# Normalising attention probabilities with a diagonal matmul instead of a transposed inverse, in a two-layer diffusion-transformer trunk

## The reference

```python
def softmax_attend(q, k, v, scale):
    s = jnp.einsum('bqhd,bkhd->bhqk', q, k, preferred_element_type=jnp.float32) * scale
    p = jax.nn.softmax(s, axis=-1).astype(v.dtype)
    return jnp.einsum('bhqk,bkhe->bqhe', p, v)
...
def gqa_sink_attend(q, k, v, sink, scale, mask=None):
    ...
    p = jax.nn.softmax(jnp.concatenate([s, sk], axis=-1), axis=-1)[..., :-1]
    return jnp.einsum('bhgqk,bkhd->bqhgd', p.astype(v.dtype), v)
```

## Time and profile before

| what | value |
|---|---|
| time, median of 3 runs | 4492.41 us (4491.73 to 4493.24) |
| time of the profiled execution | 4492.41 us |
| its span | 4490.5 us |
| instructions | 53404 |
| PE busy | 3760.7 us (84%) |
| DVE busy | 1731.2 us (39%) |
| ACT busy | 1438.4 us (32%) |

### The profile page before, as it was taken

The page is one execution under the profiler, slowest core; times in us unless marked ns, Lnnn a source line. Parts: engine busy times, 40 slices in busy tenths (PEclk is TensorE's granted clock), DMA queues, the critical chain, the costliest instruction groups (busy, mean ns, idle before and its releaser), DMA issues. The chain is left out here.

```text
span 4490.5 us, 53404 instructions
## 1 busy us (share of the span) xinstructions
PE 3760.7 (84%) x19419; PEld 2939.3 (65%) x19419; DVE 1731.2 (39%) x2448; ACT 1438.4 (32%) x2009; POOL 1196.2 (27%) x552
## 2 busy tenths in 40 slices
PE   4969987886869899998999877668867689999897
PEld 0137866776747688887877563346646568888676
DVE  0015211885761322223544404345547513223343
ACT  0035431674540411111322505544434322111222
POOL 0003322423402233332422221121111124444221
PEclk9979988998979999999999989779989899999998
DMA  5761212004423211112544222220010231222345
GB/s 171 268 206 53 69 66 83 24 30 89 101 84 116 81 62 64 61 61 71 199 168 161 70 68 57 71 70 27 27 40 20 84 133 61 79 71 70 128 169 171
DMA packets 330332, 415.65 MB, mean 93 GB/s; under 512 B 68974, under 2 KB 237534, under 8 KB 330046
## 3 DMA queue, kind: packets, MB, share of 16 engines
q1 hardware_dynamic: 300158, 327.40, 23.0%
q10 hardware_dynamic: 30016, 86.16, 5.3%
HBM read 315.95 MB, written 98.04 MB: 92 GB/s over the span
## 5 line engine op out<-in xcount | busy, mean ns | idle before, releaser
L567 PE MATMUL up_acc<-fa_act_h,up_w_hi 128*128 128x512 f32 (+1 forms) x1760 | 651.1, 370 | 27.2 <-DVE fa_act_l L508 27.2
L567 PE MATMUL up_acc<-fa_act_l,up_w_hi 128*128 128x512 f32 (+1 forms) x1760 | 649.5, 369 | 0.0
L567 PE MATMUL up_acc<-fa_act_h,up_w_lo 128*128 128x512 f32 (+1 forms) x1760 | 648.8, 369 | 0.0
L544 POOL TENSOR_TENSOR up_w_hi<-up_w_raw,ONES 128x1024 fp32r<-128x1024 f32 x88 | 210.9, 2396 | 747.0 <-PE up_acc L567 665.2
L962 DVE SCALAR_TENSOR_TENSOR up_conv<-up_acc,PRM,up_conv 128x1023 f32<-128x1023 f32 (+1 forms) x132 | 130.1, 1013 | 692.3 <-ACT up_conv L946 692.3
L567 PEld LDWEIGHTS up_acc<-fa_act_h,up_w_hi 128*128 128x128 f32 x1760 | 333.0, 189 | 87.7 <-issue 19.9
L1054 PE MATMUL dn_acc<-dn_h_hi,dn_w_hi 128*128 128x512 f32 (+1 forms) x880 | 331.6, 377 | 61.1 <-DVE dn_h_lo L1097 59.9
L567 PEld LDWEIGHTS up_acc<-fa_act_h,up_w_lo 128*128 128x128 f32 x1760 | 332.7, 189 | 55.7
L567 PEld LDWEIGHTS up_acc<-fa_act_l,up_w_hi 128*128 128x128 f32 x1760 | 333.1, 189 | 54.9
L946 ACT ACTIVATE up_conv<-up_acc,PRM 128x1280 f32<-128x1280 f32 (+1 forms) x88 | 115.8, 1316 | 767.9 <-PE up_acc L567 767.9
L1054 PE MATMUL dn_acc<-dn_h_lo,dn_w_hi 128*128 128x512 f32 (+1 forms) x880 | 328.8, 374 | 0.0
(11 more groups left out here) (353 smaller groups left out, 7843.7 us busy)
## 6 DMA issues: line engine op xcount, KB each, us to landing
dn_w_raw<-in_ffn_down SPq DMA_DIRECT2D x110, 512.0 KB, 3.3
ada_w<-in_ada_w SPq DMA_DIRECT2D x24, 2048.0 KB, 7.9
up_w_raw<-in_ffn_up SPq DMA_DIRECT2D x88, 512.0 KB, 3.8
dn_h_raw<-H SPq DMA_DIRECT2D x88, 256.0 KB, 3.4
H<-up_conv ACTq DMA_DIRECT2D x22, 640.0 KB, 2.9
H<-up_conv ACTq DMA_DIRECT2D x22, 512.0 KB, 3.5
Y<-qk_ob ACTq DMA_DIRECT2D x17, 640.0 KB, 3.0
na_bias<-RPB SPq DMA_DIRECT2D x80, 128.0 KB, 4.6
```

What stands on the lines that cost most here:

```text
L544: pool.tensor_tensor(W.hi[:, s, :, 0:mw], W.raw[:, s, :, 0:mw], ones[:, 0:mw].unsqueeze(1).broadcast_to([P, W.kt, mw]), ALU.mult)\
L567: t = pe.matmul(acc[0:mw, s, a - t0:b - t0], w[:, s, k, 0:mw], x[:, k, a - a0:b - a0], start=(k == 0 and w is W.hi and x is act_h), stop=( ...
```

## The change

Where `nw` is 2, the tiles `inv` and `inv_t`, the semaphore `spread` and the function `normalize` go. DVE now makes, for each tile and head, a 128x128 matrix `diag` with the reciprocals on its diagonal (identity times the reciprocal, one scalar for each partition). PE's "p" job multiplies each block of `PR` by `diag` in an f32 matmul, where it was a transpose through the identity, so that what comes out is transposed and normalised. It waits for `weighted[e]`, which `diag` raises, where it waited for `exped[e]`. An "o" job is then only the values, and its bank is copied plainly by ACT or DVE according to its parity. In `values` the loop over the two heads is now outside and the loop over the key blocks inside. In da (`nw` is 1) the operations stay as they are.

```diff
--- before.py
+++ after.py
@@ -1157,9 +1157,7 @@
         PR = st.sb("PR", [P, npr, 2, smax])
         PT = st.sb("PT", [P, nw, kmax, 2 * gs * P])
         if nw == 2:
-            NRB = 8
-            inv = st.sb("inv", [P, NRB, P])
-            inv_t = st.sb("inv_t", [P, 2, gs * P])
+            diag = st.sb("diag", [P, 2, 2, P])
         opar = 2
         ob = st.sb("ob", [P, opar, NTL * P])
         stat = st.sb("stat", [P, 2, 8])
@@ -1178,7 +1176,6 @@
         scored, maxed, exped, weighted = st.sems("scored"), st.sems("maxed"), st.sems("exped"), st.sems("weighted")
         t_ready, t_free = st.sems("t_ready", NB), st.sems("t_free", NB)
         chain, sink_exp, inverted = st.sem("chain"), st.sem("sink_exp"), st.sem("inverted")
-        spread = st.sem("spread")
         stored = st.sem("stored")
         block = st.block()
 
@@ -1379,15 +1376,17 @@
                                                 G.IDENT[:, :])
                         last.then_inc(t_ready[bank], 1)
                     else:
-                        if diff:
-                            pe.wait_ge(weighted[e], a + 1)
-                        else:
-                            pe.wait_ge(exped[e], a + 1)
+                        pe.wait_ge(weighted[e], a + 1)
                         t = tiles[a % NTL]
                         for x, k in enumerate(c):
                             col, _, ln = t.kts[k]
-                            last = pe.transpose(tb[0:ln, bank, x * P:(x + 1) * P], PR[:, a % npr, e, col:col + ln],
-                                                G.IDENT[:, :])
+                            w = PR[:, a % npr, e, col:col + ln]
+                            o = tb[0:ln, bank, x * P:(x + 1) * P]
+                            if diff:
+                                last = pe.transpose(o, w, G.IDENT[:, :])
+                            else:
+
+                                last = pe.matmul(o, w, diag[:, a % 2, e, :], start=True, stop=True)
                         last.then_inc(t_ready[bank], 1)
                     job[0] += 1
 
@@ -1406,14 +1405,10 @@
                 c0 = pt_cols(u * NTL + members[0])[0]
                 c1 = c0 + len(members) * P
                 t = tiles[members[0]]
-                if nw == 2:
-                    for y, x in enumerate(range(u * NTL + members[0], m + 1)):
-                        pe.wait_ge(inverted, x + 1)
-                        pe.transpose(tb[:, bank, (gs + y) * P:(gs + y + 1) * P], inv[:, x % NRB, :], G.IDENT[:, :])
-                for k, (_, vt, ln) in enumerate(t.kts):
-                    for e in range(nw):
-                        h = slice(0, P) if diff else slice(e * 64, e * 64 + 64)
-                        vc = slice(u // 2 * 64, u // 2 * 64 + 64) if swa else h
+                for e in range(nw):
+                    h = slice(0, P) if diff else slice(e * 64, e * 64 + 64)
+                    vc = slice(u // 2 * 64, u // 2 * 64 + 64) if swa else h
+                    for k, (_, vt, ln) in enumerate(t.kts):
                         last = pe.matmul(tb[h, bank, 0:c1 - c0], V[0:ln, 0 if swa else u % 2, vt, vc], PT[0:ln, e, k, c0:c1],
                                          start=k == 0, stop=k == len(t.kts) - 1)
                 last.then_inc(t_ready[bank], 1)
@@ -1431,30 +1426,11 @@
                         scores(n, half, jobs[:early(n, half)])
                     turn(jobs[early(n, half):])
 
-        def normalize(eng, copy, gn, bank, use):
-
-            u, g = divmod(gn, len(groups))
-            w = len(groups[g]) * P
-            if copy == "act":
-                eng.wait_ge(t_ready[bank], use + 1)
-                if gn >= 2:
-                    wait_freed(eng, "o", gn - 2)
-                eng.activation(inv_t[:, gn % 2, 0:w], tb[:, bank, gs * P:gs * P + w], ACT.Copy).then_inc(spread, 1)
-                return
-            eng.wait_ge(spread, gn + 1)
-            if u >= opar:
-                eng.wait_ge(stored, 16 * (u - opar + 1))
-            eng.tensor_tensor(ob[:, u % opar, groups[g][0] * P:(groups[g][-1] + 1) * P], tb[:, bank, 0:w],
-                              inv_t[:, gn % 2, 0:w], ALU.mult).then_inc(t_free[bank], 1)
-
         def evacuate(eng, copy, jobs, job):
 
             for what, a, e, c in jobs:
                 bank, use = job[0] % NB, job[0] // NB
                 job[0] += 1
-                if what == "o" and nw == 2:
-                    normalize(eng, copy, a, bank, use)
-                    continue
                 if bank % 2 != (0 if copy == "act" else 1):
                     continue
                 eng.wait_ge(t_ready[bank], use + 1)
@@ -1537,10 +1513,11 @@
                     link(dve.tensor_tensor(s, s, stat[:, p, 6:8], ALU.add))
                 link(dve.reciprocal(s, s))
                 if not diff:
-                    if m >= NRB:
-                        wait_ready(dve, "o", group_no(m - NRB))
-                    dve.tensor_copy(inv[:, m % NRB, :].rearrange("p (e d) -> p e d", e=2),
-                                    s.unsqueeze(2).broadcast_to([P, 2, 64])).then_inc(inverted, 1)
+                    for e in range(2):
+                        if m >= 2:
+                            wait_ready(dve, "p", m - 2, e)
+                        dve.tensor_scalar(diag[:, p, e, :], G.IDENT[:, :], stat[:, p, 2 + e:3 + e], None, ALU.mult)\
+                            .then_inc(weighted[e], 1)
                     return
                 link(dve.tensor_scalar(stat[:, p, 2:3], stat[:, p, 2:3], G.LINV[:, 0:1], None, ALU.mult))
                 dve.tensor_scalar(stat[:, p, 3:4], stat[:, p, 3:4], G.NLAM[:, 0:1], None, ALU.mult).then_inc(inverted, 1)
```

## The result

The changed kernel takes 4644.84 us (median of 4 runs, 4643.67 to 4648.3) against 4492.07 us before (median of 4 runs): a ratio of 1.0342, with a 95% interval of 1.033 to 1.0354. That is 153 us slower where 206 us were forecast, inside the range of 4634 to 4784 us.

The account below looks back on a forecast made before the run. PE was taken to bound the kernel, busy 84% of the span. Its added work, 93.3 us in na, 135.8 in ma and 62.7 in sw, 291.8 together, less 85.5 hidden in idle time, gave 4699 us, range 4634 to 4784.

Parts of the forecast that it names:

- PE bounds the stages: In na, ma and sw PE is busiest, leaving only 114.0 us idle in which extra PE work can hide.
- the second instruction: Probability blocks: each f32 matmul with diag is two PE instructions, 0.110 us more than a transpose, 153.1 us over 1392.
- The exchanged loops: In values, heads outside end the overlap of two heads' matmuls: 48.2 us in na, 68.8 ma, 32.7 sw.
- Rival (a): In values PE overlaps the heads despite the order, or pairs are something else: 4549 us; chance 0.09.
- Three quarters of PE's idle time: In na, ma and sw the added PE work fills 85.5 of 114.0 us idle.
- rival (c): No idle PE time is filled, since waits only move: all 291.8 us added, 4784 us or more; chance 0.05.
- The clock: PE was granted 0.97, 0.95 and 0.93 of full speed in na, ma, sw; at most 36 us to be had.
- (d): PE with fewer gaps keeps full clock and all idle time fills: 4634 us, edge of the main case's 0.82.
- 10.9: PE's 104 transposes of inv in na, ma and sw disappear, giving back 10.9 us.
- DVE and ACT at nothing: Their changed work per tile costs nothing under PE's cover; without cover at most 31 us over 104 tiles.
- the new wait at nothing: Transposes waiting for weighted[e] instead of exped[e] cost nothing, as DVE makes diag one turn before PE wants it.
- By stage: Stage lengths change by about +74 us in na, +103 in ma and +30 in sw.

Follow-up runs that it names:

- ident_matmul: The kernel before with its probability transposes made as f32 matmuls against the identity, old normalising kept: 4564.83 us, ratio 1.0167.
- order_only: The kernel before with only the two loops of values exchanged (heads outside, key blocks inside): 4569.22 us, ratio 1.0173.
- diag_only: The changed kernel with the loops of values back in the old order (key blocks outside, heads inside): 4535.22 us, ratio 1.01 to the kernel before.
- no_norm: The kernel before without the division by the sums in na, ma and sw, output copied plainly: 4416.45 us, ratio 0.9833.
- late_multiply: The kernel before, but output and transposed inverse leave the bank in one copy and DVE multiplies a turn later: 4445.24 us, ratio 0.9898.
- scale_dve: The kernel before without its old normalising; DVE instead scales the exponentials in place before PE's transposes: 4492.6 us, ratio 1.0005.

## Why the prediction was right, point by point

**PE bounds the stages, and the second instruction costs 0.110 us.** Right. Measured were 0.113 in ma, 0.12 to 0.14 in na and 0.11 in sw: 72.3, 58 and 33 us, about 163 where 153.1 stood. ident_matmul shows that it is this price and not the wait.

**The exchanged loops cost 149.7 us on PE.** The mechanism was right, the term too large. Measured were 16 x 3.50 = 56.0 us in ma (68.8 forecast), 16 x 1.79 + 16 x 0.92 = 43.4 in na (48.2), and in sw 24 x 0.70 + 8 x 0.49 = 20.7 (32.7): 120 us. The 8 context tiles of na, whose heads have only four instructions each, paid nothing. I had let nothing overlap, while at each change of heads the last four instructions of head 0 still share their slots with the first four of head 1. The 16 values of na with a block of 64 rows are the exception: with the heads outside that block is the last of head 0, stands at the change, and no pair is left at all. Rival (a), no price for the order, is refuted by order_only.

**Three quarters of PE's idle time is filled, 85.5 us.** It was 114.0 - 33.6 = 80.4 by the rows. Right, and rival (c) falls.

**The clock.** This term I mis-sized as much as the loops: I put it at zero in the sum and kept it for the edge of the range. By the clock's rows the time lost at the lower of its two levels (1.2 GHz) was at most 212 x 0.03 + 329 x 0.05 + 185 x 0.07 = 35.8 us before, and is 281 x 0.01 + 180 x 0.02 = 6.4 us after. Counting only the time in which PE was busy at that level, 64.4 us before and 11.5 after, half of the difference, 26 us, was had of the 36 us of (d). What brings it is not shown. That the denser work of PE does is argued from the stretches here, and the experiments do not bear it out as a plain rule: from the first to the last matmul of values in sw, ident_matmul was granted 1.00 with PE idle for 18.0 of 173.8 us, and diag_only 0.96 with PE idle for 6.3 of 157.4 us.

**Summed with what was measured:** 163 + 120 - 10.9 - 80.4 - 26 = 166 us, against 153 measured. Idle time is counted from modelled ends, which come late: a matmul lasts 0.273 us in the rows where the pace is 0.1075, so each idle time is some 0.16 us longer than counted. PE idled for more than 20 ns 125 times in the three stretches before and 39 times after, so another 86 x 0.16 = 14 us of idle time were filled. With this estimate the sum is 152 us.

**DVE and ACT at nothing, the new wait at nothing.** Right: one wait of 2.3 us, for a diag that stood behind POOL. The 498 ns of the spread copy in na was a mean of such cases too; without POOL beside it the copy took 0.23 us. What I under-rated is the other side, what the old normalising costs. Rows 3 gave 36.5 us of PE's waits and 10.9 of transposes; no_norm got 74 us. That is why sw came out 5 us shorter where I forecast 30 longer: PE's idle time there fell from 43.4 to 6.4 us and the clock rose from 0.93 to 0.98, and the loops cost less there than forecast; by the rows these cover nearly all of both prices.

**By stage** I forecast +74, +103 and +30 us and got +70.3, +84.6 and -3.4 by the values' rows. The stage with the most waits behind the old path was the worst estimated. The total lies near the floor of the range, since two terms erred the same way: the loops cost 30 us less than forecast and the clock gave back 26, while the second instruction cost 10 us more and 5 us less idle time was filled by the rows. The range held this only because its edge had the clock in it.

The rule of strict order from the Trainium skill, page "TensorE: Matmul & The Clock Gate", section The mechanism, would leave at most one instruction overlapped at a change of heads. The traces show four at each change, with the first of head 1 starting 0.2 to 0.7 us ahead of the last three of head 0, so in this case matmuls of different heads did not keep to that order, and the measurement decides.

## What to carry to other kernels

Before reordering a loop of matmuls, look at the spacing of neighbours from start to start: if it is half of what the moving operand needs, two narrow matmuls share the array, and the order is what lets them. An f32 product cost twice a transpose here (0.215 against 0.105 us); putting a scaling into a transpose is free only if PE has that much idle time in that very stage. And when a bank stays held for a result that two engines finish one after the other, one plain copy out of the bank and the arithmetic a turn later can be worth more than a clever way to avoid the arithmetic. When the mean of an instruction differs between stages for one shape, look at its shortest and longest and at what runs beside them before trusting the mean.

## What the hardware showed that was not expected

- Two f32 matmuls with stationary operands of 64 columns, written to different halves of the partitions, share one slot of 0.1075 us (128 moving columns) or 0.215 us (256). At a change of halves four instructions (two calls) overlap, with 128 and with 256 moving columns alike: blocks of four instructions keep 99% of the pace (4.52 against 4.47 us for 40), blocks of eight 81% (5.50), two blocks of twenty 56% (7.97).
- A key block of 64 rows is dear with the heads outside: 28 matmuls, four of them with 64 rows, take 3.62 us where 24 without them take 2.38, so 1.24 us for four instructions more. All 28 start alone, and at each change between 128 and 64 rows some 0.2 us pass from start to start. With the heads inside it was 1.83 against 1.46.
- A DVE instruction of 128 or more columns from SBUF to SBUF that began beside a running POOL instruction ended only after it, without exception in the multiply of late_multiply, the scalings of scale_dve, the spread copy before and diag after the change: the multiply of 128x128 took 285 ns without POOL and up to 3030 ns with it, the scaling of 832 columns 0.64 us and up to 3.08. The multiply that read one operand from PSUM took 290 to 292 ns either way.
